# Turning normalised activations with a diagonal, filler products in TensorE's waits, and weight slots moved inside two scans of a two-block layer

## The reference

```python
def rmsnorm(x, w):
    y = xf * lax.rsqrt(jnp.mean(xf * xf, axis=-1, keepdims=True) + EPS)
    return (y * w).astype(x.dtype)
# block 2: causal convolution, then silu, of the SSD's inputs
xbc = jax.nn.silu(causal_dwconv(mb_xbc, mb_conv_w[l], mb_conv_b[l]))
# mLSTM: s = q k^T times a decay, per head; h = s v / denom
s = jnp.einsum('bthd,bshd->bhts', qc, kc) * jnp.exp(logD - m_t[..., None])
# SSD: per head y = (C B^T * L) x; then rmsnorm over 4 groups of channels
y_intra = jnp.einsum('bhts,bshp->bthp', CB * L, xdt)
```

## Time and profile before

| what | value |
|---|---|
| median of 3 runs | 1178.35 us (1177.29 to 1178.81) |
| the profiled execution: its own time | 1177.84 us |
| its span, first to last instruction | 1176.1 us |
| TensorE busy | 1108.1 us, 94% |
| VectorE, ScalarE busy | 757.1 us (64%), 605.9 us (52%) |
| mean granted TensorE clock | 0.977 |

### The profile page before, as it was taken

One profiled execution on the slowest core, in us unless ns is written; L12 is line 12 of the kernel. 1 busy time (PEld: TensorE's weight loads), 2 busy tenths in 40 slices (PEclk: granted clock), 3 DMA queues, 4 the chain that ended last, 5 costly groups with the idle time before them and its releaser, 6 DMA issues. The chain is left out here.

```text
span 1176.1 us, 22504 instructions
## 1 busy us (share of the span) xinstructions
PE 1108.1 (94%) x9384; PEld 1050.0 (89%) x9384; DVE 757.1 (64%) x988; ACT 605.9 (52%) x784; POOL 0.2 (0%) x4
## 2 busy tenths in 40 slices
PE   6999999998999998999897899899998998999997
PEld 6899998978999997899897899889997988999996
DVE  6356666676555555788687535964546767777775
ACT  5465545346444444678464624645454445554554
POOL 0000000000000000000000000000000000000000
PEclk9999999999999998999898899999999999999999
DMA  7432434454555553335343233343443454554550
GB/s 287 177 109 109 179 133 155 179 206 152 189 179 178 183 194 123 144 144 180 108 145 109 101 115 144 134 153 117 171 162 126 179 183 160 181 208 181 178 179 37
DMA packets 26967, 184.39 MB, mean 157 GB/s; under 512 B 3064, under 2 KB 3592, under 8 KB 5128
## 3 DMA queue, kind: packets, MB, share of 16 engines
q1 hardware_dynamic: 26312, 181.38, 43.0%
q10 hardware_dynamic: 576, 1.85, 0.5%
HBM read 182.17 MB, written 1.05 MB: 156 GB/s over the span
## 5 line engine op out<-in xcount | busy, mean ns | idle before, releaser
L281 DVE TENSOR_TENSOR wlo<-raw,whi 128x2048 fp32r<-128x2048 f32 x170 | 388.9, 2291 | 228.2 <-ACT whi L274 223.8
L286 PE MATMUL pp<-XH,whi 128*128 128x256 f32 x1696 | 487.0, 287 | 5.7 <-DVE P L404 3.2
L286 PE MATMUL pp<-XL,whi 128*128 128x256 f32 x1696 | 482.2, 284 | 0.0
L286 PE MATMUL pp<-XH,wlo 128*128 128x256 f32 x1696 | 481.8, 284 | 0.0
L274 ACT ACTIVATE whi<-raw 128x2048 fp32r<-128x2048 f32 x170 | 323.8, 1910 | 61.6 <-PE pp L286 42.5
L286 PEld LDWEIGHTS pp<-XH,whi 128*128 128x128 f32 x1696 | 327.5, 193 | 11.9 <-DVE P L404 3.8
L286 PEld LDWEIGHTS pp<-XL,whi 128*128 128x128 f32 x1696 | 327.6, 193 | 0.7
L286 PEld LDWEIGHTS pp<-XH,wlo 128*128 128x128 f32 x1696 | 327.5, 193 | 0.0
L286 PE MATMUL pp<-Y,whi 128*128 128x256 f32 x480 | 87.2, 283 | 0.4 <-DVE HF L419 0.2
L1590 ACT ACTIVATE Y<-P 128x256 fp32r<-128x256 f32 x44 | 18.4, 419 | 132.7 <-DVE P L1623 132.7
L286 PEld LDWEIGHTS pp<-Y,whi 128*128 128x128 f32 x480 | 75.1, 192 | 0.9 <-DVE HF L419 0.5
(11 more groups left out here) (298 smaller groups left out, 1296.3 us busy)
## 6 DMA issues: line engine op xcount, KB each, us to landing
raw<-stream SPq DMA_DIRECT2D x170, 1024.0 KB, 4.8
P<-gains ACTq DMA_DIRECT2D x3, 512.0 KB, 3.4
X<-xt SPq DMA_DIRECT2D x2, 512.0 KB, 4.6
out<-P SPq DMA_DIRECT2D x4, 256.0 KB, 2.0
C<-consts SPq DMA_DIRECT2D x1, 345.5 KB, 11.8
P<-rows_w ACTq DMA_DIRECT2D x1, 272.0 KB, 2.8
U<-poolw SPq DMA_DIRECT2D x1, 256.0 KB, 10.5
PC<-cols SPq DMA_DIRECT2D x1, 177.0 KB, 5.4
```

Of the source, the lines that this page charges most:

```text
L281: dve.tensor_tensor(wlo[:, slot, :], raw[:, slot, :], whi[:, slot, :].bitcast(F32), ALU.subtract).then_inc(lo_ready, 1)
L286: done = pe.matmul(dst, a, b, start=first and n == 0, stop=last and n == 2, **kw)
```

## The change

1. The first pair's load is cut in halves; its split on ScalarE and VectorE too (`first_hi`, `first_lo`), and `first_pair` waits for each half where it needs it. VectorE no longer waits for the columns before turn 0.
2. `scale_dve` no longer scales x. It scales the identity (`diagonal_scale`, one 128x128 operation per half), and `turn_pe` multiplies x, as stationary operand, by that diagonal: 16 plain float32 products instead of 16 transposes.
3. Ahead of each turn TensorE does passes whose result nobody reads (`idle_passes`): 18 of 384 columns, then 27, 27 and 8 of 256.
4. The order of operations around the norms changes: table loads for the root come earlier (norms 3 and 6), `post_dve` computes a bias before two gains, norm 5 adds and squares in the order in which sums come, the last norm multiplies by the gain ahead of the scale and shares its four scalings between VectorE and ScalarE.
5. mLSTM: TensorE takes two slots ahead of the first scores instead of one; ScalarE and VectorE take one more slot ahead of their loops over heads.
6. SSD: the slot of head 0 goes, and one is added behind the last head: on TensorE ahead of the sums of squares, on ScalarE ahead of the squares, on VectorE behind the gate's product.

```diff
@@ -240,8 +240,10 @@
         sp.dma_start(C[:, 0:CLEVEL], consts[:, 0:CLEVEL]).then_inc(S("consts_loaded"), 16)
+        sp.dma_start(raw[:, 0, 0:PW // 2], stream[0, :, 0:PW // 2]).then_inc(S("first_arrived"), 16)
         sp.dma_start(PC[:, :], cols).then_inc(S("cols_loaded"), 16)
-        for p in range(RING):
+        sp.dma_start(raw[:, 0, PW // 2:], stream[0, :, PW // 2:]).then_inc(arrived[0], 16)
+        for p in range(1, RING):
@@ -256,8 +258,8 @@
             load(p, p % RING)
-        for n, (h, c) in enumerate(CHUNKS):
-            sp.wait_ge(S("result_ready"), n + 1)
+        for h, c in CHUNKS:
+            sp.wait_ge(S(f"result_ready{h}{c}"), 1)
@@ -280,6 +282,19 @@
+    def first_hi(act):
+
+        act.wait_ge(S("first_arrived"), 16)
+        act.activation(whi[:, 0, 0:PW // 2], raw[:, 0, 0:PW // 2], ACT.Copy).then_inc(S("first_hi_ready"), 1)
+        act.wait_ge(arrived[0], 16)
+        act.activation(whi[:, 0, PW // 2:], raw[:, 0, PW // 2:], ACT.Copy).then_inc(hi_ready, 1)
+
+    def first_lo(dve):
+
+        for ready, done, at in ((S("first_hi_ready"), S("first_lo_ready"), slice(0, PW // 2)), (hi_ready, lo_ready, slice(PW // 2, PW))):
+            dve.wait_ge(ready, 1)
+            dve.tensor_tensor(wlo[:, 0, at], raw[:, 0, at], whi[:, 0, at].bitcast(F32), ALU.subtract).then_inc(done, 1)
@@ -293,6 +308,8 @@
                     pe.wait_ge(S(need), 4 * rewrite + k // 2 + 1)
+                if rewrite == 0 and need == "x_hi" and k % 4 == 0:
+                    pe.wait_ge(lo_ready if k else S("first_lo_ready"), 1)
@@ -304,7 +321,8 @@
...
-        pe.wait_ge(lo_ready, p + 1)
+        if rewrite != 0:
+            pe.wait_ge(lo_ready, p + 1)
@@ -561,9 +579,11 @@
-    def norm_act(act, n, use=None, loaded=False, updated=None):
-
-        order = CHUNKS if use is None else (ORDER_OUT if use in (0, 2) else ORDER_DOWN)
+    def norm_act(act, n, use=None, loaded=False, updated=None, order=None):
+
+        order = order or (CHUNKS if use is None else (ORDER_OUT if use in (0, 2) else ORDER_DOWN))
+        if n in (3, 6):
+            load_sqrt(act)
@@ -575,8 +595,6 @@
                            ACT.Square, accum_out=stat(n, 2 * h + c)).then_inc(S("norm_partial"), 1)
-            if i == 0 and use in (1, 3):
-                load_sqrt(act)
@@ -593,36 +611,77 @@
+    def post_gain(dve, n, use, h, c):
+
+        dve.wait_ge(S("norm_partial"), 4 * n + (ORDER_OUT if use in (0, 2) else ORDER_DOWN).index((h, c)) + 1)
+        gain = words(POST_GAIN[n], 0, D)[:, c * 512:c * 512 + 512]
+        return mark(dve, dve.tensor_tensor(scaled(h, c), acc(h, c), gain, ALU.mult))
+
+    def post_add(dve, n, h, gained):
+
+        for c in range(2):
+            settled(dve, gained[c])
+            dve.scalar_tensor_tensor(chunk(h, c), scaled(h, c), stat(n, 8 + h), chunk(h, c), ALU.mult, ALU.add)\
+               .then_inc(S("x_updated"), 1)
...
-        gain = words(POST_GAIN[n], 0, D)
         dve.wait_ge(S("gain_loaded"), 16 * (n // 2 + 1))
-        written = {}
-        for i, (h, c) in enumerate(ORDER_OUT if use in (0, 2) else ORDER_DOWN):
-            dve.wait_ge(S("norm_partial"), 4 * n + i + 1)
-            written[h, c] = mark(dve, dve.tensor_tensor(scaled(h, c), acc(h, c), gain[:, c * 512:c * 512 + 512], ALU.mult))
-            if c == 0:
-                norm_bias(dve, n, h, i)
-                continue
-            norm_scale(dve, n, h)
-            settled(dve, written[h, 1])
-            for k in range(2):
-                dve.scalar_tensor_tensor(chunk(h, k), scaled(h, k), stat(n, 8 + h), chunk(h, k), ALU.mult, ALU.add)\
-                   .then_inc(S("x_updated"), 1)
-
-    def add_dve(dve, use):
-
-        for i, (h, c) in enumerate(CHUNKS):
-            wait_acc(dve, use, (ORDER_OUT if use in (0, 2) else ORDER_DOWN).index((h, c)))
-            dve.tensor_tensor(chunk(h, c), chunk(h, c), acc(h, c), ALU.add).then_inc(S("x_updated"), 1)
+        if use == 0:
+            first = [post_gain(dve, n, use, 0, 0)]
+            norm_bias(dve, n, 0, 0)
+            second = [post_gain(dve, n, use, 1, 0)]
+            norm_bias(dve, n, 1, 1)
+            first.append(post_gain(dve, n, use, 0, 1))
+            norm_scale(dve, n, 0)
+            post_add(dve, n, 0, first)
+            second.append(post_gain(dve, n, use, 1, 1))
+        else:
+            first = [post_gain(dve, n, use, 0, 0)]
+            norm_bias(dve, n, 0, 0)
+            first.append(post_gain(dve, n, use, 0, 1))
+            norm_scale(dve, n, 0)
+            post_add(dve, n, 0, first)
+            norm_bias(dve, n, 1, 2)
+            second = [post_gain(dve, n, use, 1, 0), post_gain(dve, n, use, 1, 1)]
+        norm_scale(dve, n, 1)
+        post_add(dve, n, 1, second)
+
+    def add_dve(dve, use, h, c):
+
+        wait_acc(dve, use, (ORDER_OUT if use in (0, 2) else ORDER_DOWN).index((h, c)))
+        dve.tensor_tensor(chunk(h, c), chunk(h, c), acc(h, c), ALU.add).then_inc(S("x_updated"), 1)
+
+    def diagonal_scale(dve, n, h):
+
+        norm_scale(dve, n, h)
+        dve.tensor_scalar(scale_of(h), ident, stat(n, 8 + h), None, ALU.mult).then_inc(S("x_scaled"), 1)
...
             norm_bias(dve, n, h, 2 * h)
-            norm_scale(dve, n, h)
-            for c in range(2):
-                dve.tensor_scalar(scaled(h, c), chunk(h, c), stat(n, 8 + h), None, ALU.mult).then_inc(S("x_scaled"), 1)
+            diagonal_scale(dve, n, h)
+
+    def last_gain(dve, h, c):
+
+        dve.wait_ge(S("x_updated"), 12 + 2 * h + c + 1)
+        dve.tensor_tensor(scaled(h, c), chunk(h, c), words(POST_GAIN[6], c * 512, 512), ALU.mult).then_inc(S("last_gained"), 1)
+
+    def last_scale_dve(dve, h, c):
+
+        dve.wait_ge(S("last_gained"), 2 * h + c + 1)
+        dve.tensor_scalar(scaled(h, c), scaled(h, c), stat(6, 8 + h), None, ALU.mult).then_inc(S(f"result_ready{h}{c}"), 1)
+
+    def last_scale_act(act, h, c):
+
+        act.wait_ge(S("last_gained"), 2 * h + c + 1)
+        act.wait_ge(S("last_scales"), h + 1)
+        act.activation(scaled(h, c), scaled(h, c), ACT.Copy, scale=stat(6, 8 + h)).then_inc(S(f"result_ready{h}{c}"), 1)
+
+    def scale_of(h):
+
+        return P[:, 44, h * 128:h * 128 + 128]
@@ -642,13 +701,24 @@
...
+    def idle_passes(pe, tile, width, n):
+
+        for _ in range(n):
+            pe.matmul(bank(0)[:, 0:width], tile[:, 0:128], tile[:, 0:width], start=True, stop=True)
+
+    IDLE_PASSES = {0: (RF, 384, 18), 1: (CR, 256, 27), 2: (CR, 256, 27), 3: (CR, 256, 8)}
...
+        if r == 0:
+            pe.wait_ge(S("scalars_set"), 5)
+        elif r == 1:
+            pe.wait_ge(S("masks_rounded"), 2)
+        idle_passes(pe, *IDLE_PASSES[r])
         for h in range(2):
+            pe.wait_ge(S("x_scaled"), 2 * r + h + 1)
             for j in range(KT):
-                if j % 4 == 0:
-                    pe.wait_ge(S("x_scaled"), 4 * r + 2 * h + j // 4 + 1)
-                i = pe.transpose(turned(j)[:, h * 128:h * 128 + 128], scaled(h, j // 4)[:, (j % 4) * 128:(j % 4) * 128 + 128], ident)
+                i = pe.matmul(turned(j)[:, h * 128:h * 128 + 128], X[:, h, j * 128:j * 128 + 128], scale_of(h), start=True, stop=True)
@@ -1265,6 +1335,7 @@
             act.activation(HF[:, 4 * b:4 * b + 4, :], P[:, LQ + 4 * b:LQ + 4 * b + 4, :], ACT.Tanh, scale=0.5).then_inc(S("lm_tanh"), 1)
+        st.go(1)
@@ -1373,7 +1445,7 @@
                 spread_row(pe, bank(h % 2), h, True).then_inc(S("mb_decay"), 1)
-                st.go(1)
+                st.go(1 if h else 0)
@@ -1701,7 +1776,7 @@
         st.window(*W_MLSTM)
-        st.go(1)
+        st.go(2)
@@ -1727,7 +1802,7 @@
         norm_act(act, 0, loaded=True)
-        split_hi(act, 0, 0, 0)
+        first_hi(act)
@@ -1807,12 +1882,14 @@
         st.go(3)
-        norm_act(act, 5, updated=8)
+        norm_act(act, 5, updated=8, order=ORDER_OUT)
...
         norm_act(act, 6, updated=12)
+        last_scale_act(act, 0, 1)
+        last_scale_act(act, 1, 1)
@@ -1824,11 +1901,9 @@
         dve.wait_ge(S("consts_loaded"), 16)
+        scale_dve(dve, 0)
+        first_lo(dve)
         dve.wait_ge(S("cols_loaded"), 16)
-        for h in range(2):
-            dve.wait_ge(S(f"x_loaded{h}"), 16)
-        scale_dve(dve, 0)
-        split_lo(dve, 0, 0)
@@ -1900,20 +1975,36 @@
         st.go(3)
-        add_dve(dve, 2)
-        scale_dve(dve, 5)
+        add_dve(dve, 2, 0, 0)
+        add_dve(dve, 2, 1, 0)
+        norm_bias(dve, 5, 0, 0)
+        norm_bias(dve, 5, 1, 1)
+        add_dve(dve, 2, 0, 1)
+        add_dve(dve, 2, 1, 1)
+        diagonal_scale(dve, 5, 0)
+        diagonal_scale(dve, 5, 1)
...
         ffn_side(dve, 1, dve_turn)
-        add_dve(dve, 3)
         dve.wait_ge(S("gain_loaded"), 48)
-        gain = words(POST_GAIN[6], 0, D)
-        for h in range(2):
-            norm_bias(dve, 6, h, 2 * h)
-            norm_scale(dve, 6, h)
-            for c in range(2):
```

(20 more changed lines are left out.)

## The result

The changed kernel takes 1184.73 us (median of 12 runs, 1176.38 to 1186.15), the kernel before beside it 1178.18 (1175.70 to 1178.81): the ratio over all runs is 1.004, 95% interval 1.0026 to 1.0054. It is slower, by about 0.4% (0.6% between the medians, 6.5 us). The time lies 0.7 us above the range, where the rival "the clock falls at every wait" had put it. The 12 runs lie in three groups: two at 1176.4, three at 1178.6 to 1179.4, seven at 1184.4 to 1186.2. Their mean granted clocks go the same way: 0.983 to 0.985, 0.981 to 0.983, and 0.976 to 0.977. The profiled execution (1185.45, span 1183.5) is one of the last group.

The account below looks back on a forecast made before the run. TensorE, busy 94% of the span, was taken as the bound. Terms -0.9 - 1.5 - 4.5 - 2.7 + 8.5 + 1.6 = +0.5 against the profiled 1177.84 gave 1178.3 us; range 1170 to 1184, 8 times in 10.

Parts of the forecast that it names:

- the clock falls at every wait: Rival: half clock behind the three waits for w and two in the mLSTM's tail; 1183 to 1188, central 1184; chance 17%.
- start -0.9: Start of the kernel: pair 1 starts at 21.9 instead of 22.86 us; minus 0.9 (0 to minus 1.8).
- turn 2 -0.8: Second turn: earlier table load and the diagonal let XH start at 468.35 instead of 469.13; minus 0.8.
- waits and all +8.5: mLSTM stage: new waits for w and behind the heads outweigh the removed first-scores wait; plus 8.5 (minus 5.8 to plus 9).
- falls +1.7 and +0.7: mLSTM clock falls: plus 1.7 for the three waits for w, plus 0.7 for pair 37 behind a 5 us wait.
- SSD -4.5: SSD: the moved slot covers the 3.16 us wait and the sums run at full clock; minus 4.5 (minus 3 to minus 5.1).
- end -2.7: Kernel's end: table load moves into idle time, last fused products split over two engines; minus 2.7 (minus 2 to minus 3.2).
- I take one in three: Clock term: of the three new mLSTM waits of 2.05 us, one brings a fall costing 1.7 us; plus 1.7.
- four times the price of a transpose: Turns: a skill's rule, weighed but not adopted, by which 16 products take 8 us, some 4.6 more per turn.
- The mLSTM slot pays: Rival: nothing is late in the mLSTM, so the stage gains its 5.8 us; 1162.4; chance 8%.
- The move does nothing in the SSD: Rival: the SSD's wait reappears ahead of the spread; 1182.8; chance 5%.
- the turns go cold or the products cost four times: Rival: filler does not count for the clock or the price rule holds; 2.5 us per turn, 1188; chance 3%.

Follow-up runs that it names:

- e4: Changed kernel with 14 unread passes ahead of each of three waits for w, and 40, 40 and 8 in the mLSTM's tail: 1178.12 us.
- e3: Changed kernel with 14 unread passes of 256 columns ahead of each of the three waits for w in the mLSTM heads: 1177.61 us.
- e1: Changed kernel without its added mLSTM slot, all else kept: 1164.33 us.
- e5: Changed kernel with ScalarE's catch-up behind the mLSTM's copies going one pair further: 1178.02 us.
- e6: Changed kernel with both repairs, ScalarE's catch-up one pair further and another order of tanh and convolution pairs in the mLSTM stage: 1166.46 us.
- e13: Changed kernel without the mLSTM slot, with passes ahead of TensorE's longer waits and the start's filler ahead of the wait for the constants: 1157.19 us.
- e8: Kernel before with only the SSD's slot moved from head 0 to ahead of the sums of squares: 1173.46 us.
- e10: Changed kernel with mLSTM slot, repaired order and catch-up, and passes ahead of TensorE's longer waits except the first scores: 1159.71 us.
- e9: Changed kernel without the added mLSTM slot, with unread passes ahead of TensorE's longer waits except the tail's: 1159.30 us.
- e12: Changed kernel, mLSTM slot kept as put in, with passes ahead of TensorE's longer waits and the three waits for w: 1170.63 us.
- e7: Changed kernel without the added mLSTM slot, with the start's filler put ahead of the wait for the constants: 1166.38 us.

## Why the prediction was wrong, step by step

| part | predicted | profiled executions | what failed |
|---|---|---|---|
| up to the mLSTM (start -0.9, turn 1 -0.3, turn 2 -0.8) | -2.0 | -0.1 | gains real, lost to falls |
| mLSTM stage (waits and all +8.5, falls +1.7 and +0.7) | +10.9 | +15.1 | the falls |
| behind it (SSD -4.5, turn 3 -0.4, end -2.7, clock -0.8) | -8.4 | -7.6 | nothing of weight |
| sum | +0.5 | +7.4 | |

**The mLSTM's order of events: right.** Three waits for `w` were put at 2.05 us and are 1.8; the tail's at 5.3, 5.3 and 1.2 (11.8), and are 5.2 and 3.6 (8.8); VectorE's gaps were put at 3 us and are 2.92 and 2.93. The stage without any half clock (e4) is 7.9 us longer than before, against plus 8.5.

**The step that failed is the clock, "I take one in three".** It fell behind all three waits for `w`, once for 6.8 us and twice for 3.4, and in the tail for 3.4 and 6.8. e3 prices those at `w` at 7.0 us, where the sum had 1.7; all falls of the stage together are 7.2 (144.4 less e4's 137.2), where it had 2.4. "One in three" had no row behind it: the one row named, the 2.1 us wait of L1360, had a fall behind it. The trace of before has six waits between 1.8 and 2.2 us. Behind three of them the granted clock was at 0.50 within 2.3 us (waits that ended at 183.5, 499.4 and 788.6 us); behind the others (254.4, 635.3 and 976.9) it was not; after the one at 635.3 it came only in the next wait, at 638.2. Half of three falls at 1.7 us would have been plus 2.6, still far from 7.0: that all three would bring a fall, the first of double length, the rows could not tell. The rival "the clock falls at every wait" had the time, and 17%. Its rule, that the fall "decides from a wait of about 2.0 us on", does not hold: here 1.8 us brought it, and in e1 3.03 us did not. What decides stays open.

**The second half of the failure is a term that was not in the sum:** falls in stages that the change does not touch. Pair 1 came 2.0 us earlier, not 0.9 (the constants were there at 6.15, not 6.9; the filler took 5.2 us where 5.3 was taken, and `XH` began at 13.65, not 14.6; in e1 and e3 the same filler took 6.0 us and pair 1 came at 21.7, as forecast). Turn 1 gave 0.1 for 0.3, turn 2 0.95 for 0.8. At the entry 0.1 us of all this was left, for 2.0 forecast. Two waits show where it went. TensorE waits at the same place in both kernels, before (first line) and after:

```profile
107.54 0.67 PE L819 MATMUL pm<-P 128*128 128x256 f32 x2 [1.54 <-issue]
105.47 1.06 PE L889 MATMUL pm<-P 128*128 128x256 f32 x2 [1.53 <-ACT P L967]
```

Before, the clock stayed at 1.00 there; after, it was 0.50 from 105.6 to 109.1. And behind the 2.1 us wait for the columns it was 0.50 for 6.8 us (498.2 to 505.0) instead of 3.4 (501.7 to 505.2). In the stretches above the change shows 0.83, 0.84 and 0.80 where e1, whose code is the same up to there, shows 0.91, 0.92 and 0.90. Six kernels with equal code up to the entry (after, e1, e3, e4, e5, e6) reach it at 659.2, 654.4, 654.5, 659.8, 659.4 and 659.2 us: 5 us between equal programs. Their pair 1 starts at 20.86, 21.71, 21.77, 21.28, 21.00 and 20.85 us, as the start's filler took 5.1 to 6.0: the two that start latest enter the stage earliest. So a few tenths of a microsecond at the start go with 5 us later on, not in the direction of the gain; that they cause it is not shown. The clocks of the three groups of runs fit the same reading. With passes ahead of the waits e13 keeps its early start. The whole miss adds up: 4.2 us in the stage (falls +4.8, waits -0.6), 1.9 ahead of it, 0.8 behind.

**SSD and end: right.** The wait reappeared nowhere; e8 gives 4.4 for 4.5. The end gave 2.5 for 2.7. The fall at the SSD's head is gone, though its wait of 2.1 us is still there (803.59 us). **Turns:** the products take 3.73 to 3.84 us for 16, as costed (3.4) plus the drain; a diagonal takes VectorE 0.29, where 0.2 was taken. They kept this pace with the filler and fell to 0.39 to 0.41 each without it. The rule weighed there, four times the price of a transpose, is refuted by these rows: 0.23 us each with the drain, against 0.12.

**The rivals.** "The mLSTM slot pays" would have been 1162.4; even repaired it does not: e6 and e10 show that a slot ahead of the first scores only moves their 3 us to the end of the stage, where VectorE is the bound. "The move does nothing in the SSD" and "the turns go cold or the products cost four times" did not come.

## What to carry to other kernels

A slot put ahead of a wait shifts the pairing of every later slot with the events of its stage, on every engine: walk the two written orders side by side behind the insertion, down to what each evacuation costs, before counting the wait as gained. Where the granted clock is at 0.50 behind TensorE's waits, fill these waits with unread products that take no longer; here, for waits of 1.5 to 3.0 us, that was worth 5 us (e9 against e1) to 14 us (e12 against the change). Mending the order comes first where it can be mended: without the slot, or with both repairs (e6), the change is 18 to 20 us faster. And judge edits by stretches of the trace as well as by medians, since falls of the clock elsewhere can move the whole by as much as the edit.

## What the chip showed that was not expected

Waits of 1.8 us (696.6, 716.9, 735.8 after the change) were each followed by half clock, and a wait of 3.03 us in e1 was not. The 1.5 us wait at 105.5 us and the 2.1 us wait at the SSD's head were followed by it in one of the two kernels only. The length of the wait alone does not decide. The Trainium skill, "TensorE: Matmul & The Clock Gate", section "HAM oscillation — how this bites in real kernels", tells of a loop whose every round starts cold because TensorE waits for data in each. The traces here agree in kind: half clock follows waits, and once the waits are filled, the granted clock is 1.00 from 490 to 776 us in e9.

Pair 1 earlier by 3.2 us gave no gain at the end (e7 against e1), and one earlier by 2.6 us gave 2.1 once the other waits were filled (e13 against e9). The likely reading is that what the clock costs depends on where the waits fall in time, and so on everything ahead of them; no experiment moved a wait by itself.
